# Chosen value rows gathered whole from a copy in DRAM laid out expert by expert, instead of in two halves from the weight stream

## What is computed

```python
def peer_ffn(h, w_q, sub_keys, expert_u, expert_v):
    ...
    q = (ht @ w_q).astype(jnp.float32).reshape(T, PEER_HEADS, 2, PEER_HALF)
    s = jnp.einsum('thpd,hpkd->thpk', q, sub_keys.astype(jnp.float32))
    top_s, top_i = lax.top_k(s, PEER_TOPK)
    ...
    def block_fn(args):
        xb, ib, gb = args
        u = jnp.take(expert_u, ib, axis=0)
        act = jax.nn.gelu(jnp.einsum('td,thkd->thk', xb, u).astype(jnp.float32))
        w = (gb * act).astype(xb.dtype)
        v = jnp.take(expert_v, ib, axis=0)
        return jnp.einsum('thk,thkd->td', w, v)
```

## Time and profile before

| | us |
|---|---|
| median of 3 runs | 3009.84 |
| lowest and highest | 3003.88, 3011.19 |
| the profiled execution, its own time | 3010.22 |
| span of its profile | 3008.4 |
| PE busy | 2899.1 (96%) |
| POOL busy | 2170.7 (72%) |
| DVE busy | 1793.9 (60%) |
| ACT busy | 812.8 (27%) |
| moved by DMA | 447.68 MB, 149 GB/s on the mean |

### The profile page before, as it was taken

How to read it: one execution, slowest core, us unless ns; L and a number is a source line. 1 busy time by engine, 2 the same in 40 slices (tenths; PEclk the granted TensorE clock), 3 DMA queues, 4 the chain that set the end, 5 groups by cost and what they waited for, 6 DMA issues and landing times.

```text
span 3008.4 us, 40272 instructions
## 1 busy us (share of the span) xinstructions
PE 2899.1 (96%) x13614; PEld 2437.7 (81%) x13614; DVE 1793.9 (60%) x2944; ACT 812.8 (27%) x1351; POOL 2170.7 (72%) x1223
## 2 busy tenths in 40 slices
PE   7999999999999999999999989999999998999997
PEld 6788877788887888888888889899998865778885
DVE  5578756221133888888890067676777667776611
ACT  3245223221011212121121133233232456232201
POOL 6843564577787698989987777878786551678876
PEclk9999999999999999999999999999999998999999
DMA  4211221233333345555545499999997320223331
GB/s 144 91 57 49 91 84 56 63 92 97 126 105 97 111 132 190 184 192 182 182 138 200 160 342 316 302 307 302 305 307 254 92 73 15 70 88 95 97 98 63
DMA packets 237070, 447.68 MB, mean 149 GB/s; under 512 B 120992, under 2 KB 137504, under 8 KB 235936
## 3 DMA queue, kind: packets, MB, share of 16 engines
q1 hardware_dynamic: 191792, 314.90, 33.4%
q0 software_dynamic: 24576, 67.20, 6.5%
q10 hardware_dynamic: 20592, 64.23, 5.5%
HBM read 385.44 MB, written 60.82 MB: 148 GB/s over the span
## 4 chain that ended last, share of the span: by engine, by line
PE 74%; POOL 14%; DVE 5%; issue 4%; DMA 1%; ACT 1%; POOLq 0%; DVEq 0%; ACTq 0%; SPq 0%
PE bank L680 18%; PE bank L682 17%; PE bank L681 17%; POOL v_rows L597 8%; POOL row_acts L605 5%; PE banks L680 2%; PE banks L682 2%; PE banks L681 2%; PE banks L831 2%; PE banks L980 2%; PE banks L793 1%; PE banks L795 1%; PE banks L794 1%; PE banks L896 1%; DMA v_rows<-weights,v_row_of_choice 1%
## 5 line engine op out<-in xcount | busy, mean ns | idle before, releaser
L547 POOL TENSOR_TENSOR w_hi<-w_raw,ones 128x1024 fp32r<-128x1024 f32 x364 | 696.9, 1915 | 656.0 <-PE bank L682 438.1
L549 POOL TENSOR_TENSOR w_lo<-w_raw,w_hi 128x1024 fp32r<-128x1024 f32 x364 | 893.8, 2455 | 28.6
L680 PE MATMUL bank<-h_hi,w_hi 128*128 128x512 f32 x2000 | 792.1, 396 | 8.1 <-DVE h_lo L1992 7.1
L682 PE MATMUL bank<-h_hi,w_lo 128*128 128x512 f32 x2000 | 779.5, 390 | 0.0
L681 PE MATMUL bank<-h_lo,w_hi 128*128 128x512 f32 x2000 | 778.5, 389 | 0.0
L680 PEld LDWEIGHTS bank<-h_hi,w_hi 128*128 128x128 f32 x2000 | 376.0, 188 | 92.5 <-DVE h_lo L1992 13.9
L682 PEld LDWEIGHTS bank<-h_hi,w_lo 128*128 128x128 f32 x2000 | 375.3, 188 | 80.2
L681 PEld LDWEIGHTS bank<-h_lo,w_hi 128*128 128x128 f32 x2000 | 376.0, 188 | 75.3 <-issue 2.2
L597 POOL DMA_INDIRECT v_rows<-weights,v_row_of_choice x256 | 297.2, 1161 | 78.0 <-issue 75.9
L1642 ACT ACTIVATE act_out_stage<-bank 128x512 f32<-128x512 f32 x128 | 76.6, 598 | 578.5 <-PE bank L682 501.9
L2537 DVE SCALAR_TENSOR_TENSOR token_sums<-v_rows,row_weights,token_sums 128x1024 f32<-128x1024 f32 x127 | 164.0, 1292 | 102.3 <-DMA v_rows<-weights,v_row_of_choice 96.9
(11 more groups left out here) (488 smaller groups left out, 5601.6 us busy)
## 6 DMA issues: line engine op xcount, KB each, us to landing
w_raw<-weights SPq DMA_DIRECT2D x430, 512.0 KB, 3.7
acts<-act_out_stage ACTq DMA_DIRECT2D x128, 256.0 KB, 2.9
v_raw<-weights SPq DMA_DIRECT2D x64, 512.0 KB, 5.2
gates<-gate_stage ACTq DMA_DIRECT2D x6, 4096.0 KB, 12.8
acts_in<-acts SPq DMA_DIRECT2D x128, 192.0 KB, 5.0
gates_in<-gates SPq DMA_DIRECT2D x128, 192.0 KB, 5.5
v_rows<-weights,v_row_of_choice POOLq DMA_INDIRECT x256, 4.4
resid<-x SPq DMA_DIRECT2D x4, 512.0 KB, 7.8
```

What stands on the lines that cost most here:

```text
L547: nc.gpsimd.tensor_tensor(w_hi[:, pair, :], w_raw[:, slot, :], one_col.to_broadcast((P, 1024)), ALU.mult).then_inc(hi_split, 1)
L549: nc.gpsimd.tensor_tensor(w_lo[:, pair, :], w_raw[:, slot, :], f32(w_hi[:, pair, :]), ALU.subtract).then_inc(split_done, 1)
L680: mm(out_, hi, rhs_hi, start=first, stop=False)
L682: return mm(out_, lo, rhs_hi, start=False, stop=last)
```

## The change

A DRAM tensor `values` of 64 MB is added, in which a V row of 1024 floats lies whole. SP fills it from `weights` with 128 DMAs from DRAM to DRAM, each one V tile of 512 KB in 256 pieces of 2 KB. From the ninth load of the early run on, one copy is issued right behind each load. For that the loops of loads are written out. POOL gathers a row by one indirect DMA of 4 KB per token instead of two of 2 KB, after a wait for all copies. DVE works out one row number per choice instead of two, with less arithmetic. The other edits (`consts_set`, `rows_ready`, `last_by_act`, `last_by_pool`, `bank_summed` for `down_summed`, `dve_step` for `choices_here`) merge semaphores, and leave the instructions and their order as they are.

```diff
+COPY_FROM = 8
...
-    v_rows = place("v_row_of_choice", [P, 2, CHOICES], S1 + 2 * KB, U32)
+    v_row = place("v_row_of_choice", [P, CHOICES], S1 + 2 * KB, U32)
...
+    values = nc.dram_tensor("values", (NKEYS, P, 2, 512), F32, kind="Internal").ap()
...
-        def four_tiles(i):
-            for s in range(RAW):
-                load(i * RAW + s, s)
+        copies = iter([(g, half, pair) for g in range(NKEYS // GROUP) for half in range(2) for pair in range(GROUP // 2)])
+
+        def copy_values():
+
+            g, half, pair = next(copies)
+            tile = weights[START["experts"] + g * (2 * GROUP) + GROUP + half * (GROUP // 2) + pair, :, :]
+            key = g * GROUP + 2 * pair
+            sp.dma_start(values[key:key + 2, :, half, :].rearrange("e p n -> p e n"),
+                         tile.rearrange("p (e n) -> p e n", e=2)).then_inc(values_copied, 16)
...
-        c.loop(1, START["w_hg"] // RAW, four_tiles)
-
+        early = [*range(RAW, START["w_hg"])]
         for name, n in (("rg", 16), ("w_hg", 8), ("w_ret", 16), ("w_out", 8), ("peer_q", 16)):
-            load_run(START[name], n)
+            early += range(START[name], START[name] + n)
+        for n, tile in enumerate(early):
+            load(tile, n % RAW)
+            if COPY_FROM <= n < COPY_FROM + NKEYS:
+                copy_values()
...
-        value_rows = weights.rearrange("i p (e n) -> (i p e) n", e=2)
+        value_rows = values.rearrange("e p half n -> (e p) (half n)")
...
-            for half in range(2):
-                pool.indirect_dma_start(
-                    out=row_slot[j % ROW_SLOTS][:, half * 512:half * 512 + 512], out_offset=None, in_=value_rows,
-                    in_offset=bass.IndirectOffsetOnAxis(ap=v_rows[:, half, j:j + 1], axis=0)).then_inc(v_row_in[j // 2 % PAIR_SLOTS], 16)
+            pool.indirect_dma_start(
+                out=row_slot[j % ROW_SLOTS][:], out_offset=None, in_=value_rows,
+                in_offset=bass.IndirectOffsetOnAxis(ap=v_row[:, j:j + 1], axis=0)).then_inc(v_row_in[j // 2 % PAIR_SLOTS], 16)
...
-        pool.wait_ge(rows_placed, 1)
+        pool.wait_ge(rows_ready, 1)
+        pool.wait_ge(values_copied, 16 * NKEYS)
...
-            ve.tensor_copy(place_u[:, 0, :], keys_of[0]).then_inc(dve_step, 1)
...
+            stt(low_f[:], keys_of[0], float(NKEYS), keys_of[1], ALU.mult, ALU.add).then_inc(dve_step, 1)
             dve.wait_ge(dve_step, c.due(dve_step, 2))
...
+            ve.tensor_copy(v_row[:], low_f[:]).then_inc(dve_step, 1)
...
-            dve.wait_ge(v_row_in[j // 2 % PAIR_SLOTS], 64 * (j // ROW_SLOTS + 1))
+            dve.wait_ge(v_row_in[j // 2 % PAIR_SLOTS], 32 * (j // ROW_SLOTS + 1))
```

More of the change, by code:

```diff
@@ L316, in build @@
     row_act_in = [sem(f"row_act_in{n}") for n in range(2)]
-    rows_placed, rows_weighted, row_summed, v_hi_ready = (sem(n) for n in (
-        "rows_placed", "rows_weighted", "row_summed", "v_hi_ready"))
+    values_copied = sem("values_copied")
+    rows_ready, row_summed, v_hi_ready = (sem(n) for n in ("rows_ready", "row_summed", "v_hi_ready"))
     raw_loaded = [sem(f"raw_loaded{n}") for n in range(RAW)]
@@ L333, in build @@
         "hi_split", "split_done", "hot_gated"))
-    choices_here, gate_copied, tok_summed = (sem(n) for n in ("choices_here", "gate_copied", "tok_summed"))
+    gate_copied, tok_summed = (sem(n) for n in ("gate_copied", "tok_summed"))
     tile_done, sq_used, lev_done, far_done, o_done = (sem(n) for n in (
@@ L356, in build @@
         "sb_exp", "df_exp", "df_pt_read", "df_o_read"))
-    dve_step, eps_set, ones_set, h_ready, bounds_shifted, f_done = (sem(n) for n in (
-        "dve_step", "eps_set", "ones_set", "h_ready", "bounds_shifted", "f_done"))
+    dve_step, consts_set, h_ready, bounds_shifted, f_done = (sem(n) for n in (
+        "dve_step", "consts_set", "h_ready", "bounds_shifted", "f_done"))
     decay_done, far_e_ready, lev_diff, far_ready, lev_ready, lev_read = (sem(n) for n in (
@@ L371, in build @@
     silu_done, gate_product, gate_hi = (sem(n) for n in ("silu_done", "gate_product", "gate_hi"))
-    down_summed, last_squared, sq_paired, last_gained, final_pool = (sem(n) for n in (
-        "down_summed", "last_squared", "sq_paired", "last_gained", "final_pool"))
+    last_by_act, last_by_pool = (sem(n) for n in ("last_by_act", "last_by_pool"))
     merged, bank_summed, conv_begun, ff_product, ff_hi_done, rstd_f_ready = (sem(n) for n in (
@@ L523, in _ @@
         store(0, 2)
-        sp.wait_ge(final_pool, 2)
+        sp.wait_ge(last_by_pool, KT // 2 + 2)
         store(5, 7)
@@ L527, in _ @@
         store(2, 4)
-        sp.wait_ge(final_pool, 3)
+        sp.wait_ge(last_by_pool, KT // 2 + 3)
         store(7, 8)
@@ L539, in _ @@
         one_col = ones[:, 0:1]
-        pool.wait_ge(ones_set, c.due(ones_set))
+        pool.wait_ge(consts_set, 2)
         def split(slot, held=2):
@@ L798, in group_tm @@
                 ins.then_inc(tile_done, 1)
-        pe.wait_ge(ones_set, c.due(ones_set))
+        pe.wait_ge(consts_set, 2)
         fresh_fm(16, 4, 1, acc_read_act, also_read=4)
@@ L1365, in down @@
                     if last and p == 1 and n < KT - 1:
-                        ins.then_inc(down_summed, 1)
+                        ins.then_inc(bank_summed, 1)
                 ins.then_inc(tile_done, 1)
@@ L1440, in root_table @@
             act.wait_ge(act_step, c.due(act_step))
-        act.wait_ge(eps_set, c.due(eps_set))
+        act.wait_ge(consts_set, 1)
         root_table()
@@ L1693, in _ @@
         act.wait_ge(gates_out, c.due(gates_out, 0))
-        act.wait_ge(rows_placed, 1)
+        act.wait_ge(rows_ready, 1)
         for k in range(2):
@@ L1926, in _ @@
             act.wait_ge(down_read, c.due(down_read))
-            fn(last_sq[:, k, :], resid[:, k, :], ACT.Square).then_inc(last_squared, 1)
+            fn(last_sq[:, k, :], resid[:, k, :], ACT.Square).then_inc(last_by_act, 1)
         def gained(k):
-            fn(bank[k + 1][:] if k < 5 else resid[:, k, :], resid[:, k, :], ACT.Copy, scale=v("final2", k)).then_inc(last_gained, 1)
+            fn(bank[k + 1][:] if k < 5 else resid[:, k, :], resid[:, k, :], ACT.Copy, scale=v("final2", k)).then_inc(last_by_act, 1)
         for k in range(4):
@@ L1999, in normed_parts @@
             dve.wait_ge(plain_read, c.due(plain_read, plain))
[L2001 to L2004, removed]
+        ve.memset(eps[:], EPS).then_inc(consts_set, 1)
+        dve.wait_ge(consts_set, 1)
+        ve.memset(ones[:], 1.0).then_inc(consts_set, 1)
+        dve.wait_ge(consts_set, 2)
         dve.wait_ge(consts_in, c.due(consts_in, 16))
@@ L2407, in place_rows @@
-            dve.wait_ge(dve_step, c.due(dve_step, 3))
-            ve.tensor_copy(place_f[:, 0:2, :], place_u[:, 1:3, :]).then_inc(dve_step, 1)
+            dve.wait_ge(dve_step, c.due(dve_step))
+            ve.tensor_reduce(tiny[:, 62:63], pick[:, :, 0], AX.X, ALU.add).then_inc(dve_step, 1)
+            dve.wait_ge(dve_step, c.due(dve_step))
+            ts(tiny[:, 62:63], tiny[:, 62:63], float(DT), None, ALU.add).then_inc(dve_step, 1)
+            stt(low_f[:], keys_of[0], float(NKEYS), keys_of[1], ALU.mult, ALU.add).then_inc(dve_step, 1)
@@ L2414, in place_rows @@
[L2414 to L2425, removed]
+            ve.tensor_copy(act_row[:], low_f[:]).then_inc(rows_ready, 1)
@@ L2529, in add_row @@
                 dve.wait_ge(row_act_in[chunk % 2], 16 * CHUNK * (chunk // 2 + 1))
-                tt_(row_w[:, col], row_act[:, col], chosen[:, 3, col], ALU.mult).then_inc(rows_weighted, 1)
-                dve.wait_ge(rows_weighted, chunk + 1)
-            dve.wait_ge(v_row_in[j // 2 % PAIR_SLOTS], 64 * (j // ROW_SLOTS + 1))
+                tt_(row_w[:, col], row_act[:, col], chosen[:, 3, col], ALU.mult).then_inc(rows_ready, 1)
+                dve.wait_ge(rows_ready, 1 + (chunk + 1))
+            dve.wait_ge(v_row_in[j // 2 % PAIR_SLOTS], 32 * (j // ROW_SLOTS + 1))
             if j == 0:
@@ L2832, in _ @@
             if n < KT - 1:
-                dve.wait_ge(down_summed, c.due(down_summed))
+                dve.wait_ge(bank_summed, c.due(bank_summed))
             else:
```

24 lines of the change are left out of this document (10 added, 14 removed).

## The result

| | us |
|---|---|
| before, median of 4 runs (lowest to highest) | 3007.95 (3003.88 to 3011.19) |
| changed, median of 4 runs (lowest to highest) | 2932.74 (2931.83 to 2933.30) |
| ratio, 95% interval | 0.975 (0.9733 to 0.9767) |
| changed, the profiled execution and its span | 2932.43, 2930.6 |

The change gains 75 us. I had forecast 2954 us, a gain of 56, and a range that ended at 2937: the direction was right and so was POOL as what set the pace; the limit that I put right behind it was not, and the range missed by 4 us.

What follows compares the result with a forecast made beforehand. POOL's issuing of gathers was taken to bound the value stage. PE could regain 69 us, but DMA engine time held the stage to 562 us: 3010.2 - 56 = 2954 us, other parts nothing. Range 2937 to 2986 us.

Steps and rivals of the forecast that it cites:

- the limit that I put right behind it: Value stage: after POOL, the DMA engines bind, since their 562 us of engine time stays; gain 56 us.
- POOL sets the pace by its number of gathers: Value stage: issuing gathers costs POOL 36.3 us a chunk against PE's 31.4; 128 fewer row gathers make it 24.7 us.
- A 4 KB gather costs POOL what a 2 KB gather does: Row gathers on POOL: cost doesn't grow with bytes, taken as 1.459 us each; upper end twice that.
- rival 2: Row gathers on POOL: 4 KB costs double, a chunk stays 36.3 us, time 3010 us; chance 0.05.
- PE gets back 69 us, the stage lasts 549: Value stage behind the opening: stalls and slow clock could come back, 69 us; the opening's 9.0 us stall stays.
- The DMA engines in that stage can't be squeezed under 562 us: Value stage: 0.91 of 618 us is engine time that stays, so stage 562 us, gain 56 us.
- What the wider pieces save, nothing: DMA engines, row gathers: 2 KB pieces aren't slower, 342 GB/s against 311 for 4 KB loads; saving taken as nothing.
- rival 4: Value stage: all comes back and engine time shrinks by the skill's rule, 2941 us; chance 0.64 together with the main forecast.
- The copies are free: Early stages: load and copy need 5.0 us of 5.4 us per dense tile, the cover is deep; nothing for PE.
- My price of 3.3 us for a copy: DMA engines: upper bound for a 512 KB copy, read and write one after the other, 1.7 + 1.6 us.
- The sum: Whole kernel: 3010.2 - 56 = 2954 us, with no correction from the profiled execution to the median.
- 1 (the queues bind at 0.95): Value stage: DMA engines bind sooner, stage 592 us, time 2984 us; chance 0.21.
- 3 (copies starve the loads): SP's queue, 70 to 940 us: copies over 3.7 us delay early loads; at 5.5 us, 3116 us; chance 0.10.

## Why the prediction was right or wrong

*POOL sets the pace by its number of gathers.* Right, and now shown from both sides: with 16 row gathers per chunk put back the gain is gone, and with seven of the eight activation gathers taken out instead it is there without the change.

*A 4 KB gather costs POOL what a 2 KB gather does.* Right here, 1.17 and 1.16 us, where I had 1.154 (1.459 with the gap behind it). In the later runs, on the one chip that has both, it is 1.25 against 1.20 to 1.23 us, and on the other two a 4 KB gather takes 1.32 to 1.38, still far from the double of rival 2.

*PE gets back 69 us, the stage lasts 549.* Right within 2: it lasts 547, since the opening's stall was 6.7 us and not 9.0.

*The DMA engines in that stage can't be squeezed under 562 us.* This is the step that failed: "I take 562: a gain of 56 us". The stage lasts 547 us, and the gain in it is 71. I took recorded engine time for work that stays. The same bytes were recorded as 0.91 x 618 = 562 us before, 0.95 x 547 = 520 us after, and 0.98 x 541 = 530 us in the run with the old layout and free POOL; the row gathers at 342, 392 and 394 GB/s. With POOL loaded again (two pieces from the copy) they were 0.86 x 655 = 563 us. So the recorded time of the same transfers is lower in the runs in which POOL doesn't hold the stage up, with pieces of 2 KB as with 4 KB; why it is, no run here isolates. Nor was a share of about 1 a limit: from 1800 to 2200 us the changed kernel holds 1.02 with PE busy throughout, and my own rows had 1.09 over 30 us. The direct evidence that I had weighed too little was SP's 299.5 us of waiting for slots. What SP showed after is still 178 us of it.

*What the wider pieces save, nothing.* Held within what a single profile of each shows: between 2 and 4 KB, with the layout equal, 0.98 x 542 and 0.97 x 538 differ by 9 us of engine time, with shares given to 0.01 (5 us), and the stage by 4 us. The Trainium skill (Perfetto Trace Analysis, DMA Optimizations) says that going from 2 KB to 4 KB can dramatically improve throughput where a kernel is DMA-bound. These two runs don't show that, and as PE is the limit in both they can't refute it either. I had given that rule the forecast's own better end (rival 4, 2941 us). The number came close, its reason didn't, so rival 4 came near by luck.

*The copies are free.* Right: none and two behind each load take the same time. My price of 3.3 us for a copy was over twice the 1.4 us that it adds, which nothing in the sum hung on.

*The sum.* 2941 us would have been the answer without the failed step. The profiled executions lie 77.8 us apart, not 71: 1.9 us came at the start, where the kernel before ran some of its first 40 us at the lower clock (0.96 granted) and the changed one didn't, and 4.6 us came behind the last arithmetic. Its last group on POOL, in the kernel before and in the changed one:

```profile
2995.24 3.72 POOL L664 TENSOR_TENSOR final<-resid,rstd 128x512 f32<-128x512 f32 x3 [5.35 <-DVE rstd L2838]
```
```profile
2922.03 3.71 POOL L675 TENSOR_TENSOR final<-resid,rstd 128x512 f32<-128x512 f32 x3 [5.35 <-DVE rstd L2836]
```

From there to the end of the span it is 13.2 us and 8.6 us, with the same instructions. Nothing in the change accounts for either; the kernel before ranges over 7 us between its runs. I had named the profiled execution's 0.4 us to the median and left it there, and the range's lower end, 2937, had no room for these 6.5 us and the 2 us by which the stage came out shorter.

*Rivals.* 1 (the queues bind at 0.95) fell: the stretch 1800 to 2200 us holds its share of 1.02 at 357 GB/s. 2 (double price on POOL) fell. 3 (copies starve the loads) is there with four copies per load and not with two; three, 1.7 + 4.2 = 5.9 us against 5.4 by the same sum, wasn't run.

## What to carry to other kernels

Where an engine that issues gathers rests only for the fixed gap between instructions (0.30 us here), count its instructions, not its bytes: fewer and larger gathers, or fewer of any kind, give the same. A DMA share near 1 isn't yet a floor: ask the issuer of the loads whether it waits for slots, and if it does, leave the engines out of the sum or in the range only. A large copy can hide beside compute-bound stages, as long as load and copies together stay under the time of a tile; here that sum told two copies, which fit, from four, which don't.

## What was unexpected in the hardware

In the first comparison the cost of an indirect gather of 128 rows on POOL doesn't grow with its bytes: in the changed kernel's profile it is 1.18 us with 4 bytes per row and 1.17 us with 4 KB. In the later profiles on other chips this holds less well: in the changed kernel's it is 1.19 us with 4 bytes and 1.38 us with 4 KB, the difference coming from a longer median and from single long gathers. All row gathers of the changed kernel, in the first comparison, then in the later one of six runs (min/median/max ns, first and last start):

```profile
L607 POOL DMA_INDIRECT v_rows<-values,v_row_of_choice x128: 932/947/1960, 1729.2 to 2223.0; - x128
```
```profile
L607 POOL DMA_INDIRECT v_rows<-values,v_row_of_choice x128: 934/1078/3904, 1728.7 to 2235.7; - x128
```

In that comparison the kernel before takes 3072 us instead of 3008, and the changed one 2945 instead of 2933. So the change is worth 127 us there and 75 here. It is tempting to put this down to the slow gathers, but the traces don't bear that out. The changed kernel's stage is 13 us longer there, and 10.5 us of that are the halt at 1765 to 1780 us, ahead of its first gather of over 2 us (at 1781.64 us). The version with the sums two units later has five gathers of 2.9 us and more, and its stage lasts 540 us. The kernel before has no trace on these chips; the nearest is the one with two pieces from the copy, which lives by POOL's pace too. It has a single gather of over 2.1 us and pays 36.4 us per chunk, as in the first comparison. What it does have is more such halts, the longest near the end of its stage (PE, from 2270 to 2320 us):

```profile
2270.00:2320.00 50.00, 26.02 (x107) 0.66 0.64 196
```

At the full rate some 286 matmuls would start there. So several of the later profiles have halts of PE, ACT and DVE in the stage that the first two don't have, and for which the profile names no releaser. What they are, and how much of the kernel before's 64 us they make, is open.

A DRAM-to-DRAM copy of 512 KB in pieces of 2 KB adds 1.4 us of engine time, less than a load of the same size into SBUF by the same view (1.7 us).
